# A decoder layer on one core: w_in loaded in pieces of 512 columns by half of the rows

## The reference

```
h = _rmsnorm(x, g_pre_mix) * (1.0 + sc1) + sh1
aq, af, ai, ag, bq, bk, bv, gate_a, gate_b = jnp.split(h @ w_in, IN_SPLITS, axis=-1)
```

## Time and profile before

| | |
|---|---|
| median of 3 runs | 1396.59 us (1395.32 to 1397.75) |
| profiled execution: time, span | 1397.93 us, 1396.2 us |
| mean granted PE clock | 0.914 |
| PE busy | 1199.3 us, 86% of the span |
| DVE, ACT, POOL busy | 527.1, 259.4, 64.5 us |
| projection's matmuls, L601 | 154.2 us busy, 576 records |
| DMA | 485.34 MB, mean 348 GB/s |
| w_in loads | 22 of 1024 KB, median 8.2 us from issue to landing |
| w_mod loads | 24 of 1024 KB, median 6.4 us |

### The profile page before, as it was taken

One profiled execution on the slowest core, in us unless ns is written; L12 is line 12 of the kernel. 1 busy time (PEld: TensorE's weight loads), 2 busy tenths in 40 slices (PEclk: granted clock), 3 DMA queues, 4 the chain that ended last, 5 costly groups with the idle time before them and its releaser, 6 DMA issues.

```text
span 1396.2 us, 22110 instructions
## 1 busy us (share of the span) xinstructions
PE 1199.3 (86%) x8926; PEld 538.9 (39%) x8926; DVE 527.1 (38%) x872; ACT 259.4 (19%) x461; POOL 64.5 (5%) x126
## 2 busy tenths in 40 slices
PE   2899999999996967979869798899986797667996
PEld 0576778887743311323213232233321232112332
DVE  1603563323354522424325344444433253232444
ACT  2000421003032211212112122222211121111222
POOL 2001010102003000000000000000000000000000
PEclk9898989878995987999989999999999899897998
DMA  9887554425458999999999999799999999999994
GB/s 299 309 305 284 191 162 139 144 85 191 141 230 325 395 428 427 428 428 427 427 428 429 428 427 427 325 389 408 410 429 429 427 428 428 426 427 427 428 429 192
DMA packets 65629, 485.34 MB, mean 348 GB/s; under 512 B 5797, under 2 KB 28698, under 8 KB 37754
## 3 DMA queue, kind: packets, MB, share of 16 engines
q1 hardware_dynamic: 57760, 460.95, 80.1%
q0 software_dynamic: 6160, 18.72, 4.3%
q10 hardware_dynamic: 1642, 4.67, 1.0%
HBM read 478.56 MB, written 5.76 MB: 347 GB/s over the span
## 4 chain that ended last, share of the span: by engine, by line
PE 54%; DMA 34%; DVE 10%; issue 1%; ACT 0%; POOL 0%; ACTq 0%; DVEq 0%; POOLq 0%
DMA big<-in_w_gate_up 23%; PE PB L990 17%; PE PB L601 10%; PE PB L1013 8%; DMA big<-in_w_down 8%; PE PB L557 2%; DVE mod L1783 2%; PE PB L618 2%; PE PB L845 2%; PE PB L869 2%; PE PB L571 2%; PE PB L783 1%; DVE mod L1777 1%; DVE mod L1780 1%; DVE mod L1776 1%
## 5 line engine op out<-in xcount | busy, mean ns | idle before, releaser
L990 PE MATMUL PB<-big,cst 128*32 128x512 f32 x3072 | 393.1, 658 | 116.2 <-DMA big<-in_w_gate_up 116.1
L990 PEld LDWEIGHTS PB<-big,cst 128*32 128x32 f32 x3072 | 99.3, 116 | 385.9 <-issue 204.2
L1776 DVE TENSOR_SCALAR mod<-PB 64x512 f32<-64x512 f32 x48 | 32.8, 683 | 481.4 <-PE PB L990 481.4
L1013 PE MATMUL PB<-big,cst 128*32 128x512 f32 x1536 | 176.6, 596 | 9.6 <-DMA big<-in_w_down 9.6
L601 PE MATMUL PB<-hTG,big 128*128 128x264 f32 x576 | 154.2, 428 | 2.8 <-DVEq L1339 2.5
L601 PEld LDWEIGHTS PB<-hTG,big 128*128 128x128 f32 x576 | 119.9, 213 | 35.8 <-issue 8.6
L1212 ACT ACTIVATE mod<-mod 64x512 f32<-64x512 f32 x48 | 30.3, 631 | 462.3 <-DVE mod L1776 462.3
L957 PE MATMUL PB<-tok,att 64*128 64x512 f32 x392 | 97.4, 615 | 0.0
L1787 DVE TENSOR_REDUCE att<-hTG 128x272 f32<-128x1088 f32 x48 | 61.7, 1286 | 78.4 <-PE PB L965 78.4
L1013 PEld LDWEIGHTS PB<-big,cst 128*32 128x32 f32 x1536 | 43.9, 109 | 119.3 <-issue 76.1
L945 PE MATMUL PB<-wide,att 128*32 128x256 f32 x1176 | 77.9, 397 | 0.0
(11 more groups left out here) (285 smaller groups left out, 1004.2 us busy)
## 6 DMA issues: line engine op xcount, KB each, us to landing
big<-in_w_gate_up SPq DMA_DIRECT2D x128, 2048.0 KB, 26.6
big<-in_w_down SPq DMA_DIRECT2D x64, 2048.0 KB, 22.8
big<-in_w_mod SPq DMA_DIRECT2D x24, 1024.0 KB, 6.4
big<-in_w_in SPq DMA_DIRECT2D x22, 1024.0 KB, 8.2
wide<-in_cache_k POOLq DMA_DIRECT2D x16, 256.0 KB, 3.3
hTG<-in_cache_v POOLq DMA_DIRECT2D x16, 256.0 KB, 3.1
big<-in_w_out SPq DMA_DIRECT2D x4, 1024.0 KB, 8.3
big<-in_state_hgrn POOLq DMA_DIRECT2D x4, 512.0 KB, 4.9
```

The costliest lines, as they stand in the source:

```text
L990: mm = pe.matmul(GU[32 * j:32 * j + 32, :], mo["xT"][:, r * P + u * M:r * P + (u + 1) * M], w[:, r * 2 * D + j * 512:r * 2 * D + (j + 1) * ...
L1013: mm = pe.matmul(DN[32 * j:32 * j + 32, :], mo["actT"][:, r * 64 + u * M:r * 64 + (u + 1) * M], w[:, r * D + half * 512:r * D + (half + 1) ...
L1776: dve.tensor_scalar(mo["glu"], GU[0:64, :], LIMIT, None, ALU.min).then_inc(S("glu_ready"), 1)
```

## The change

A piece of w_in holds 512 columns of 512 rows (four chunks k) in place of 256 columns of all 1024 rows. `in_T` goes over the halves of k outside and over the four tiles inside, so all four tiles stay open in their banks over both pieces, and `proj_full` is raised in the second half alone. The first piece's release is a new semaphore `half_used`. `in_tok` runs matmuls of 512 columns, four k in each half, and all its sample tiles at the end with both pieces; both pieces are released by its last `proj_full`, and `tok_half` is gone. The `between` steps and `two_mods` are issued behind the same number of matmuls as before.

```diff
@@ after_unit
-                if u[2] == 1:
+                if u[2] == 1 or len(names) == 3:
                     return "proj_full", PROJ[names[-1]] + 1
-                return ("proj_full", PROJ[names[1]] + 1) if len(names) == 4 else ("tok_half", 1 if u[1] == 6 else 2)
+                return "half_used", [v for v in IN_ORDER if len(IN_NAMES[v]) == 4].index(u[1]) + 1
@@ SP
-                    src = win[:, :, u[1] * 512 + u[2] * 256:u[1] * 512 + (u[2] + 1) * 256]
-                    dst = dst.rearrange("p (k n) -> p k n", k=KC)
+                    src = win[:, 4 * u[2]:4 * u[2] + 4, u[1] * 512:(u[1] + 1) * 512]
+                    dst = dst.rearrange("p (k n) -> p k n", k=4)
@@ in_T
-                for j, name in enumerate(IN_NAMES[u]):
-                    w = unit("in", u, j // 2)
-                    bank = proj_bank(name)
-                    for k in range(KC):
-                        mm = pe.matmul(bank[:, 0:T], w[:, k * 256 + (j % 2) * P:k * 256 + (j % 2 + 1) * P], hT[:, k, :],
-                                       start=(k == 0), stop=(k == KC - 1))
-                    mm.then_inc(S("proj_full"), 1)
-                    if j % 2:
-                        two_mods()
-                    if between:
-                        for step in between[j]:
-                            step[0](*step[1:])
+                for half in range(2):
+                    w = unit("in", u, half)
+                    for j, name in enumerate(IN_NAMES[u]):
+                        bank = PB[PROJ[name] % 4] if half else proj_bank(name)
+                        for q in range(4):
+                            k = 4 * half + q
+                            mm = pe.matmul(bank[:, 0:T], w[:, q * 512 + j * P:q * 512 + (j + 1) * P], hT[:, k, :],
+                                           start=(k == 0), stop=(k == KC - 1))
+                        if half:
+                            mm.then_inc(S("proj_full"), 1)
+                        elif j == 3:
+                            mm.then_inc(S("half_used"), 1)
+                        if j == 3:
+                            two_mods()
+                        if between and j % 2:
+                            for step in between[2 * half + j // 2]:
+                                step[0](*step[1:])
@@ in_tok
+                halves = []
                 for half in range(2):
                     w = unit("in", u, half)
+                    halves.append(w)
                     for c in range(2):
-                        for k in range(KC):
-                            mm = pe.matmul(banks[c][:, half * 256:(half + 1) * 256], hT[:, k, c * P:(c + 1) * P],
-                                           w[:, k * 256:(k + 1) * 256], start=(k == 0), stop=(k == KC - 1))
+                        for q in range(4):
+                            k = 4 * half + q
+                            mm = pe.matmul(banks[c][:, :], hT[:, k, c * P:(c + 1) * P], w[:, q * 512:(q + 1) * 512],
+                                           start=(k == 0), stop=(k == KC - 1))
...
-                    for j in range(2):
-                        for k in range(KC):
-                            mm = pe.matmul(banks[2][:, (2 * half + j) * NS:(2 * half + j + 1) * NS],
-                                           w[:, k * 256 + j * P:k * 256 + (j + 1) * P],
-                                           hT[:, k, TP:T], start=(k == 0), stop=(k == KC - 1))
-                    mm.then_inc(S("proj_full" if half else "tok_half"), 1)
+                    if half:
+                        for j in range(4):
+                            for k in range(KC):
+                                mm = pe.matmul(banks[2][:, j * NS:(j + 1) * NS],
+                                               halves[k // 4][:, (k % 4) * 512 + j * P:(k % 4) * 512 + (j + 1) * P],
+                                               hT[:, k, TP:T], start=(k == 0), stop=(k == KC - 1))
+                        mm.then_inc(S("proj_full"), 1)
                     two_mods()
```

## The result

The changed kernel took 1419.52 us in the median of 5 runs (1416.98 to 1421.95), the one before 1396.59 (1395.32 to 1398.55) beside it: ratio 1.0173, interval 1.0156 to 1.019. It is slower by 22.9 us between the medians, by 24.2 by the ratio. Forecast were 1414.8, in a range from 1406 to 1423. The profiled execution has a span of 1417.8 us, 21.6 more than before, at a mean granted clock of 0.907.

A forecast was written before the change was run, and what follows sets the result against it. PE was taken to bound the changed stretch, almost without gaps. Terms -0.6 + 9.1 + 6.0 + 0.5 + 3.2 = +18.2 on 1396.6 gave 1414.8 us; the 8-in-10 range was 1406 to 1423.

The forecast's parts named there:

- Part 1: Input projection: larger w_in rows and fewer matmuls save the 0.4 us wait and 0.1 per token unit, together -0.6 us.
- Part 2: in_T's new order on PE: tiles become full later within each unit, but PE waits for no bank there; no cost.
- Part 3: Unit 10: gb4 full later delays ACT's Ln and Exp and DVE's sample_state(3); PE waits before out_sample(3), +9.1 us.
- Part 4: Unit 6: late release of its first piece delays the next loads, +6.0 us; 5.4 on idle queues, 7 with shared engines.
- Part 5, sample block: Units 6 and 2: half clock from 64 thin records together, up to 2.6 us, against 1.1 given back; +0.5 us taken.
- Part 5, behind the idle stretch: Unit 10: after 9.1 us idle, half clock on out_sample(3), 1.7 us, and the matmuls behind it, 1.5; +3.2 us.
- the signs: Behind unit 6: SP issues two mods and two w_in in a row at about 116 us.
- The rival that the expert loads swallow the delay: Expert loads: their start not bound to PE, so the front's stalls cost nothing; 1394.9 us, chance 0.04.
- one of the two waits isn't there: Units 6 and 10: without unit 6's load wait 1409 us, without unit 10's wait 1402 us; chance 0.07.
- the costly end: Units 6 and 10: stores and cache pages share with all loads, clock stays low; 1425 us, half-way 1421, chance 0.13.

The follow-up runs named there:

- Experiment 3: Changed kernel with branch b's Ln and Exp before take(gb4) and sample tiles accumulated in two halves, first piece released behind the first: 1395.34 us, ratio 0.9991.
- Experiment 1: Changed kernel with branch b's Ln and Exp on ACT put before take(gb4) instead of before take(gb5): 1407.51 us, ratio 1.0081.
- Experiment 4: Only the feature-major units (in_T) changed, units 6 and 2 as in the kernel before: 1408.3 us, ratio 1.0079.
- Experiment 7: Kernel before with branch b's Ln and Exp on ACT before take(gb6) instead of before take(gb5): 1406.83 us, ratio 1.0077.
- experiment 9: Changed kernel with ACT's stores of v and k issued behind take(aq1), some 20 us later: 1419.99 us, ratio 1.0158.
- experiment 11: Changed kernel with Ln and Exp before take(gb4), sample tiles in two halves, and eight-column matmuls laid between the 512-column ones: 1386.41 us, ratio 0.9934.
- Experiment 5: Only the token-major units (in_tok) changed, the nine feature-major ones as in the kernel before: 1409.31 us, ratio 1.0102.
- experiment 2: Changed kernel with sample tiles of units 6 and 2 accumulated in two halves, first piece released behind the first half: 1408.01 us, ratio 1.0075.
- experiment 8: Changed kernel with out_sample(3) issued behind gb7, before the logit constants, instead of between gb5 and gb6: 1419.56 us, ratio 1.0178.

## Why the prediction was right

Time, sign and both mechanisms came as forecast; the sum was 18.2, the median moved 22.9. The measured time lies inside the range, but near its upper end. Both waits and the sample block were put too low; only the term behind the idle stretch came out lower than forecast, net. By its steps:

- *Part 1*, -0.6: the wait of 0.4 at unit 5 went. Experiment 3 shows no more, -0.1% at an interval of the same size.
- *Part 2*, no cost: in0 to unit 10 took 195.0 us for 195.6, and in_T alone had no wait but unit 10's. q1's packets in the first 420 us fell from 30186 to 18769, as said.
- *Part 3*, +9.1: +9.8 in the trace, a wait of 9.4. Experiments 1, 4 and 7 show it in three ways. Of the 0.7 more, 0.3 lie in the wait (9.37) and 0.4 in the clock, which I had taken as unchanged: outer(3) and the tile behind it took 2.72 and 6.42 us (at 333.5 and 336.2) for 1.98 and 5.52, the unit's first tile 3.72 for 4.96.
- *Part 4*, +6.0: the term was short, +7.6. I had put it nearer the idle queue (5.4) than the shared one (7); with the stores taken out of the burst (experiment 9) it was 5.6, that is 11.2 less 5.6, so the sharing should have been taken in full. The burst came at 120.24, not about 116, since the sample block before it ran longer, and it was two mods, one w_in and a third mod where the signs named two mods and two w_in.
- *Part 5, sample block*, +0.5: the step that was most off. It was +2.9, just above the 2.6 that I had worked out for a second half at half clock and then not taken, because I set unit 2's fall against it. Even so 2.6 less 1.1 would have been +1.5, and the prediction gives no reason for less. Unit 2 gave back 0.1 (28.25 us for 28.35).
- *Part 5, behind the idle stretch*, +3.2: +4.8 at first. out_sample(3) added the 1.7 foreseen, but the matmuls behind it 3.0 (6.76 us for 3.81) in place of 1.5. Then 2.7 came back in the head sums and the merge, which in the kernel before had the half clock themselves (0.50 at 344 to 350) and now ran at full. Net +2.1; the part that came back was not foreseen. The Trainium skill's rule ("TensorE: Matmul & The Clock Gate", Why this matters for your kernels) held for the gap of 9.4 us (1.00 at 346:350, 0.50 at 354:356) and, in experiment 11, for one of 3.18 (1.00 at 128:130, 0.50 at 132:134). The gap of 5.5 us does not test it, since the clock stood at 0.50 before it began.
- *The rival that the expert loads swallow the delay* is refuted by the gate_up load at 401.16. Experiments 4 and 5 refute that one of the two waits isn't there.
- *The range*: its upper end, 1423, is called half-way to the costly end, but half-way from 1414.8 to 1425 is 1420, and the rival puts it at 1421. The measured 1419.5 would have been just inside that too.

## What to carry to other kernels

When a tile is finished later though the work is the same, look on the engine that empties it for everything that stands behind that take: an unrelated chain queued there comes late by the same amount, and one line moved ahead of the take cures it. When a buffer is held over a second half, the load to look at is the next in the issuer's order, not the buffer's own next user. Thin matmuls laid between wide ones can keep the clock up; measure it each time. Between 512-column matmuls it did so in both units, between 264-column ones in two groups of four. And it gained time only where the next load was already there: in unit 6 a wait for weights took all of it.

## What the runs showed of the hardware

- A block of 64 eight-column records was followed by a granted clock of 0.50 from within the block, through the waits behind it, until 3 us into the next 264-column tile (112 to 137 us, changed kernel). The same records laid four to every wide matmul left it at 1.00 in units 6 and 2 (88 to 128 and 164 to 192 us, experiment 11).
- The same block of 32 such records left the clock up in one kernel and not in another: the mod matmuls behind unit 6's first block took 1.92 us in experiment 2, 3.64 in experiment 3.
- An idle stretch of 3.18 us in a row at full clock was followed by 0.50, and the tile behind it took 6.46 us for 3.83 (experiment 11).
- With 3.7 us of work shifted into a wait, the half clock fell on the matmuls behind instead, and 1.4 us were gained in the trace (experiment 8, one trace against one).
- Issued together beside 1 MB of stores, the first two of four 1 MB loads took 6.9 us in the median to land, the w_in piece behind them 12.3 and a third mod piece 14.3 (changed kernel, 120 to 122.4 us), against 5.5 and 8.3 in the earlier trace rows.
